# x kept in DRAM between the halves of a feed-forward, its memory used to stage operands; the start of the feed-forward reordered

## The reference

```python
x = x + o @ w_o                                   # end of the cross-attention
h = jnp.square(jax.nn.relu(rms_norm(x, g_f) @ w1))    # w1: 1024 x 4096
return x + h @ w2                                 # w2: 4096 x 1024
```

## Time and profile before

| | |
|---|---|
| median of the runs | 2828.93 us |
| the profiled execution | 2825.01 us |
| its span | 2823.2 us, 51395 instructions |
| TensorE | 2499.7 us busy, 89% |
| VectorE | 1434.8 us busy, 51% |
| ScalarE | 851.6 us, 30% |
| GpSimd | 472.6 us, 17% |
| mean granted clock of TensorE | 0.937 of full |
| feed-forward | from about 2035 to 2806 us of the span |

### The profile page before, as it was taken

The page is one execution under the profiler, slowest core; times in us unless marked ns, Lnnn a source line. Parts: engine busy times, 40 slices in busy tenths (PEclk is TensorE's granted clock), DMA queues, the critical chain, the costliest instruction groups (busy, mean ns, idle before and its releaser), DMA issues. The chain is left out here.

```text
span 2823.2 us, 51395 instructions
## 1 busy us (share of the span) xinstructions
PE 2499.7 (89%) x21934; PEld 2252.0 (80%) x21934; DVE 1434.8 (51%) x2399; ACT 851.6 (30%) x1417; POOL 472.6 (17%) x411
## 2 busy tenths in 40 slices
PE   5998799978996789987999999988879998599888
PEld 5995789837993455556999999976779998599888
DVE  4445566442326677542122324434586765555675
ACT  4324232211124344452121213223332232232332
POOL 1001333203103233210000000000132323122221
PEclk7997899978996999998999999999989999799999
DMA  8320100045112111165111114031024344433432
GB/s 292 104 81 15 18 4 4 4 156 126 41 55 73 45 60 60 60 250 181 46 45 46 45 46 144 8 108 57 23 64 161 127 161 149 165 107 99 153 116 84
DMA packets 181589, 252.81 MB, mean 90 GB/s; under 512 B 19190, under 2 KB 147618, under 8 KB 172681
## 3 DMA queue, kind: packets, MB, share of 16 engines
q1 hardware_dynamic: 170547, 185.53, 21.4%
q0 software_dynamic: 9888, 61.87, 6.2%
q10 hardware_dynamic: 926, 2.12, 0.2%
HBM read 195.56 MB, written 58.28 MB: 90 GB/s over the span
## 5 line engine op out<-in xcount | busy, mean ns | idle before, releaser
L3599 PE MATMUL ps<-ff_operand_high,ff_weight_parts 128*128 128x264 f32 x1024 | 298.6, 292 | 58.7 <-DVE ff_operand_low L3741 19.1
L3601 PE MATMUL ps<-ff_operand_high,ff_weight_parts 128*128 128x264 f32 x1024 | 295.9, 289 | 0.0
L3600 PE MATMUL ps<-ff_operand_low,ff_weight_parts 128*128 128x264 f32 x1024 | 295.8, 289 | 0.0
L3599 PEld LDWEIGHTS ps<-ff_operand_high,ff_weight_parts 128*128 128x128 f32 x1024 | 198.2, 194 | 62.2 <-issue 62.0
L3599 PE MATMUL ps<-ff_sums_high,ff_weight_parts 128*128 128x264 f32 x768 | 221.7, 289 | 27.7 <-DVE ff_hidden L3765 12.5
L3601 PE MATMUL ps<-ff_sums_high,ff_weight_parts 128*128 128x264 f32 x768 | 220.0, 286 | 0.0
L3600 PE MATMUL ps<-ff_sums_low,ff_weight_parts 128*128 128x264 f32 x768 | 219.7, 286 | 0.0
L3600 PEld LDWEIGHTS ps<-ff_operand_low,ff_weight_parts 128*128 128x128 f32 x1024 | 198.4, 194 | 0.0
L3601 PEld LDWEIGHTS ps<-ff_operand_high,ff_weight_parts 128*128 128x128 f32 x1024 | 198.2, 194 | 0.0
L3086 PE MATMUL ps<-xn_h,me_gate_w_high 128*128 128x352 f32 x576 | 186.8, 324 | 6.1 <-DVE me_gate_w_low L3152 6.1
L3087 PE MATMUL ps<-xn_l,me_gate_w_high 128*128 128x352 f32 x576 | 185.5, 322 | 0.0
(11 more groups left out here) (737 smaller groups left out, 6908.0 us busy)
## 6 DMA issues: line engine op xcount, KB each, us to landing
ff_raw<-in_w_ff SPq DMA_DIRECT2D x64, 512.0 KB, 5.1
ff_staged<-hidden_operands SPq DMA_DIRECT2D x28, 1056.0 KB, 5.0
hidden_operands<-ff_hidden SPq DMA_DIRECT2D x16, 1056.0 KB, 4.3
hidden_operands<-ff_hidden_sums SPq DMA_DIRECT2D x16, 792.0 KB, 7.0
me_gate_w_raw<-in_w_in SPq DMA_DIRECT2D x23, 512.0 KB, 3.9
pj_raw<-in_w_in SPq DMA_DIRECT2D x13, 512.0 KB, 4.6
xn_high<-xn_h POOLq DMA_DIRECT2D x1, 4224.0 KB, 14.3
xn_low<-xn_l POOLq DMA_DIRECT2D x1, 4224.0 KB, 25.4
```

The costliest lines, as they stand in the source:

```text
L3599: e.matmul(o[:, cols], wring[:, r, 0, k, :], high(i)[:, k, cols], start=first, stop=False, skip_group_check=True)
L3600: e.matmul(o[:, cols], wring[:, r, 0, k, :], low(i)[:, k, cols], start=False, stop=False, skip_group_check=True)
L3601: mm = e.matmul(o[:, cols], wring[:, r, 1, k, :], high(i)[:, k, cols], start=False, stop=k == 3, skip_group_check=True)
```

## The change

x is stored to DRAM (`x_dram`) in unit 0 of the feed-forward, and its memory becomes four more staging buffers (`x_staged`). Operands 0 to 3 of the down half are loaded into them in unit 8; 4 uses `staged[0]`, 5 and 6 use two of the four again, 7 and later alternate as before. x comes back in four loads (`back`), each when the buffers on it have been converted, and the first group's takes into x wait for them. `hidden_after` gives other places for the conversions. SP issues the staged loads of the group changes before the second weight half of the unit, and the first two of the group after next behind it. Two of the four running tiles of P1's results (`g1`) change place. At the start, the squares of the last 288 columns and their sums are made in `stage_mem` block by block between the output products, as are the rest of the second third's scaling and unit 0's weight sums; VectorE forms all operand sums, and the first half of product 0 no longer waits for the last third.

```diff
-        at = 7 * (NPAIR + 4 * g - 1) + i + 2
-        if n in (1, 2):
-            at += n
-        if n in (3, 4, 5, 6):
-            at = 7 * NPAIR + n - 2
-        if at == q:
+        late = (0, 1, 2, 3, 6, 9, 11) if g == 0 else (0, 1, 3, 5, 7, 8, 10)
+        if 7 * (NPAIR + 4 * g - 1) + late[i] == q:
             out.append(n)
     return out
+
+
+def weight_sums(e, raw, tmp, s_ws, u):
+
+    A = lambda i, j: raw[:, (2 * u + j) % HALVES, :, P * i:P * i + P]
+    e.tensor_tensor(tmp[0][:, :, :], A(1, 0), A(1, 1), ALU.add).then_inc(s_ws, 1)
+    e.wait_ge(s_ws, 4 * u + 1)
+    e.tensor_tensor(tmp[1][:, :, :], tmp[0][:, :, :], A(0, 0), ALU.subtract).then_inc(s_ws, 1)
+    e.tensor_tensor(A(1, 0), A(0, 0), A(1, 0), ALU.subtract).then_inc(s_ws, 1)
+
+
+def weight_last_sum(e, raw, tmp, s_ws, u):
+
+    e.wait_ge(s_ws, 4 * u + 2)
+    e.tensor_tensor(tmp[2][:, :, :], raw[:, (2 * u + 1) % HALVES, :, 0:P], tmp[1][:, :, :], ALU.subtract).then_inc(s_ws, 1)
 
...
-    squares = alloc("end_squares", O, [P, KD, NL])
+    x_staged = [alloc(f"x_staged{b}", at - 4 * KD * T + 16 * NH * b, [P, 4, NH]) for b in range(4)]
...
     t1 = alloc("first_product", K.cst_at + 512, [P, NH])
-    g1 = [outB[:, m, :] for m in range(3)] + [t1[:, :]]
-    tmp = [alloc("weights_s1", K.cst_at + 2656, [P, 4, P]), alloc("weights_s2", K.cst_at + 2656 + 2048, [P, 4, P]),
-           alloc("weights_s4", K.utail_at, [P, 4, P])]
+    g1b = alloc("first_product_sums", slab - 2048 - 4 * NH, [P, NH])
+    g1 = [t1[:, :], g1b[:, :], outB[:, 0, :], outB[:, 1, :]]
...
-    PARTS = (slice(0, 2 * THIRD), slice(2 * THIRD, NH))
-    stage_of = lambda n: 0 if n < 3 else (n - 3) % 2
+    PARTS = (slice(0, 2 * THIRD), slice(2 * THIRD, NH), slice(0, NH))
+    in_x = lambda n: n < 7 and n != 4
+    slot = lambda n: (n if n < 4 else n - 3) if in_x(n) else (0 if n == 4 else n % 2)
+    stage_home = lambda n: x_staged[slot(n)] if in_x(n) else staged[slot(n)]
+    stage_count = lambda n: 16 * (1 + sum(in_x(l) == in_x(n) and slot(l) == slot(n) for l in range(n)))
...
 
             def stage(n):
                 g, i = divmod(n, 7)
-                if n == 0:
+                if n < 4:
+                    e.wait_ge(s_xd, 16)
+                    e.wait_ge(s_n, 1)
+                    e.wait_ge(s_sa[0], 32)
+                    e.wait_ge(s_sa[1], 32)
+                    e.wait_ge(s_sb, 64)
+                elif n == 4:
                     e.wait_ge(s_sa[0], 16 * (NPAIR // 2))
-                elif n == 4:
+                elif n in (5, 6):
+                    e.wait_ge(s_x2, n - 2)
+                elif n == 7:
                     e.wait_ge(s_sa[1], 16 * (NPAIR // 2))
                     e.wait_ge(s_sb, 16 * NPAIR)
-                elif n < 4:
-                    e.wait_ge(s_x2, n)
+                elif n == 8:
+                    e.wait_ge(s_x2, 5)
                 else:
                     e.wait_ge(s_x2, n - 1)
-                e.dma_start(staged[stage_of(n)][:, :, :], kept[:, g, KEPT[i], :, :]).then_inc(s_st[stage_of(n)], 16)
-
+                e.dma_start(stage_home(n)[:, :, :], kept[:, g, KEPT[i], :, :]).then_inc((s_xs if in_x(n) else s_st)[slot(n)], 16)
+
+            def back(m):
+                e.wait_ge(s_x2, (1, 2, 6, 7)[m])
+                e.dma_start(x[:, 2 * m:2 * m + 2, :], xkept[:, 2 * m:2 * m + 2, :]).then_inc(s_xr[m], 16)
+
+            xkept = K.x_dram.rearrange("p (k n) -> p k n", k=KD)
             for u in range(NU):
-                if 1 <= u <= NPAIR:
+                if 1 <= u < NPAIR:
                     store(u - 1)
                 if 2 * u + 3 < 2 * NU:
                     half(2 * u + 3)
+                if u == 0:
+                    e.dma_start(xkept, x[:, :, :]).then_inc(s_xd, 16)
+                if u == 8:
+                    for n in range(4):
+                        stage(n)
+                if u == NPAIR - 1:
+                    stage(4)
+                    back(0)
+                    stage(5)
+                if u == NPAIR:
+                    back(1)
+                    store(NPAIR - 1)
+                if u == NPAIR + 1:
+                    back(2)
+                g, m = divmod(u - NPAIR, 4)
+                if u >= NPAIR and m == 3 and g < 3:
+                    for n in range(7 * (g + 1) + 2, 7 * (g + 2)):
+                        stage(n)
                 if 2 * u + 4 < 2 * NU:
                     half(2 * u + 4)
                 if u == NPAIR - 1:
-                    for n in range(4):
+                    stage(6)
+                if u == NPAIR + 1:
+                    back(3)
+                    stage(7)
+                    stage(8)
+                if u >= NPAIR and m == 3 and g < 2:
+                    for n in range(7 * (g + 2), 7 * (g + 2) + 2):
                         stage(n)
-                if u >= NPAIR:
-                    g, m = divmod(u - NPAIR, 4)
-                    if u == NPAIR:
-                        for n in range(4, 9):
-                            stage(n)
-                    elif m == 3 and g < 3:
-                        for n in range(7 * (g + 1) + 2, min(7 * (g + 2) + 2, 28)):
-                            stage(n)
 
         @block.gpsimd
         def _(e):
...
+                weight_sums(e, raw, tmp, s_ws, u)
                 if u:
...
+                weight_last_sum(e, raw, tmp, s_ws, u)
+
             for u in range(1, NU):
                 sums(u)
 
         @block.tensor
         def _(e):
-            def product(q):
+            def product(q, halves=(0, 1)):
                 u, i = divmod(q, 7)
                 o, r = bank(u, SLOT[i]), q % RINGW
-                for z in range(2):
+                for z in halves:
                     cols = slice(NH // 2 * z, NH // 2 * z + NH // 2)
                     for k in range(4):
                         first = k == 0 and i in (P1, P6, P5)
                         e.matmul(o[:, cols], wring[:, r, 0, k, :], high(i)[:, k, cols], start=first, stop=False, skip_group_check=True)
                         e.matmul(o[:, cols], wring[:, r, 0, k, :], low(i)[:, k, cols], start=False, stop=False, skip_group_check=True)
                         mm = e.matmul(o[:, cols], wring[:, r, 1, k, :], high(i)[:, k, cols], start=False, stop=k == 3, skip_group_check=True)
...
+                    e.wait_ge(s_z, 1)
+                    product(0, (0,))
                 if u == 0:
                     e.wait_ge(s_x1, i + 1)
                 elif u >= NPAIR and (u - NPAIR) % 4 == 0:
                     e.wait_ge(s_x2, 7 * ((u - NPAIR) // 4) + i + 1)
                 room(u, i)
-                product(q)
+                product(q, (1,) if q == 0 else (0, 1))
 
         @block.scalar
         def _(e):
...
                 e.wait_ge(s_mm, 7 * (NPAIR + 4 * g - 1) + i + 1)
-                e.activation(high(i), staged[b][:, :, :], ACT.Copy).then_inc(s_xh2, 1)
-
-            e.activation(squares[:, :, :], x[:, :, end], ACT.Square).then_inc(s_sq, 1)
-            e.wait_ge(s_n, 1)
+                e.activation(high(i), stage_home(n)[:, :, :], ACT.Copy).then_inc(s_xh2, 1)
+
             operand_high(P1, 0)
             weights_high(0)
-            operand_high(P2, 0)
-            weights_high(1)
             e.wait_ge(s_var, 1)
             e.activation(rstd[:, end], rstd[:, end], ACT.Sqrt).then_inc(s_root, 1)
+            operand_high(P2, 0)
             operand_high(P3, 0)
+            weights_high(1)
+            weights_high(2)
+            e.wait_ge(s_n, 1)
+            operand_high(P1, 1)
             e.wait_ge(s_T2, 1)
-            operand_high(P6, 0)
-            operand_high(P5, 0)
+            operand_high(P6, 2)
+            operand_high(P2, 1)
+            e.wait_ge(s_T4, 1)
+            operand_high(P4, 2)
+            operand_high(P5, 2)
             e.wait_ge(s_T3, 1)
-            operand_high(P7, 0)
-            e.wait_ge(s_T4, 1)
-            operand_high(P4, 0)
-            e.wait_ge(s_n, 2)
-            operand_high(P1, 1)
-            weights_high(2)
-            operand_high(P2, 1)
+            operand_high(P7, 2)
             operand_high(P3, 1)
-            e.wait_ge(s_TB, 1)
-            for i in (P6, P7, P5, P4):
-                operand_high(i, 1)
 
             for q in range(NQ):
                 u, i = divmod(q, 7)
...
@@ -3809,6 +3831,8 @@
                         e.drain()
                     return
                 v = u - NPAIR
+                if g == 0 and i == P6:
+                    e.wait_ge(s_xr[m], 16)
                 if i == P5:
                     e.wait_ge(s_td, 7 * v + P7 + 1)
                 elif i == P3:
...
 
-            for k in range(4, KD):
-                mm = normed_third(e, K, xn, x, rstd, 1, k)
-            e.drain().then_inc(s_n, 1)
+            def first_sum(to, a, b, z):
+                c = PARTS[z]
+                return e.tensor_tensor(whole(to)[:, :, c], whole(a)[:, :, c], whole(b)[:, :, c], ALU.subtract)
+
+            first_sum(P5, P7, P1, 0)
```

(60 more changed lines are left out.)

44 lines of the change are left out of this document (13 added, 31 removed).

## The result

The changed kernel took 2781.06 us (median of 4 runs, 2777.24 to 2785.46) and the kernel before 2827.44 (4 runs, 2824.36 to 2832.48). The ratio is 0.9835, 95% interval 0.981 to 0.9859. It is faster by 46; 2770 was forecast. The profiled execution took 2777.24 against 2825.01.

A forecast was written before the change was run, and what follows sets the result against it. TensorE was taken to be 89% busy, leaving only idle and half-clock time. Head 3, unit 8 -1, seam 36 and group changes 19 sum to 57 off 2825, 2768 profiled, given as 2770; range 2756 to 2792 for 8 in 10.

The forecast's parts named there:

- What bounds the kernel: TensorE 89% busy, only idle and half-clock time winnable; at three seam and group-change waits VectorE stood at conversions lacking staged operands.
- Seam: Between up and down halves, units 15 to 17: staging in x's memory cuts the excess from 50.2 to 14, gain 36 us.
- rival 2: Seam and head: GpSimd's weight sums block VectorE's conversions for whole sets; seam gain 27, head's gone, 2780; chance 0.14.
- Head: Feed-forward's start: sums moved ahead and a shorter VectorE chain up to the first unit's P4 product; gain 3 us.
- Unit 8: Middle of the up half: four loads of 1056 KB fill the queue, so GpSimd's weights come late; loss 1 us.
- Group changes: Three later changes in the down half: earlier, spread conversions remove the gap, a late weight half remains at two; gain 19 us.
- Rival 1: Group changes: late loads make conversions slip in the two buffers' cycle, so no gain there; 2787 to 2789; chance 0.13.
- Rival 3: Down units: weight halves stand behind staged loads and x's blocks in the queue, starving weights; slower, 2840; chance 0.03.
- Rival 4: Unit 8: late stores of the group or x hold up its loads in SP; time as Rival 3, no chance of its own.

The follow-up runs named there:

- e1_no_x: Changed kernel without x's way to DRAM and back; all operands staged in the two buffers at the earlier places: 2808.52 us, ratio 0.994.
- e4_filled: Changed kernel with matmuls nobody reads put into five of TensorE's waits, before products 2, 5, 108, 114 and 118: 2772.13 us, ratio 0.9803.
- e6_spread: Changed kernel with the four loads into x's memory issued one each in units 5 to 8, not all in unit 8: 2784.53 us.
- e11_guarded: Changed kernel with the loads into x's memory two each in units 7 and 8, issued once GpSimd has begun the next unit's weight sums: 2781.25 us.
- e8_tuned: Changed kernel with e2_order's queue order, e6_spread's loads, and one conversion later at the seam and in later groups: 2769.37 us, ratio 0.9797.
- e2_order: Changed kernel with the first two staged loads of the group after next issued one unit later, behind that unit's weight halves: 2773.86 us, ratio 0.9808.
- e7_old_places: Changed kernel with e2_order's queue order, but the later groups' conversions at the places of the kernel before: 2797.38 us.
- e9_all: Changed kernel with e2_order's order, e8_tuned's later conversions, e11_guarded's loads and unread matmuls in five TensorE waits: 2753.56 us, ratio 0.9757.

## Why the prediction was right, point by point

The forecast time of 2770 is 11 under the measured one, within the range, and the sign and, in the main, the mechanism were right. By its own steps:

**What bounds the kernel.** Right for the most part. The idle time at the seam was mainly VectorE at conversions whose operand had not landed; e1_no_x, which keeps all but that staging, is back at 83.0 of 91.05. One of the three readings was wrong. Behind the 15.86 VectorE did not stand at a conversion but, for 11.36 us, at the take of P1, whose tile was still being stored (the row of 2432.64). The change frees that tile, and this is worth the other 8.0; the prediction has no term for it and put the whole gain down to the staging.

**Seam, 36, measured 34.7.** The written order followed gave releases at 2387.3, 2397.7, 2409.6 and 2423.4; measured 2387.39, 2399.15, 2412.05 and 2427.66, waits of 9.85 us in all against 9.4. The excess over 40.8 is 15.5: the 9.85, three falls of the clock at 1.5 where one at 1.6 and 3 us of GpSimd were charged, and 1.1 that shows as neither. That the sum came out is in part luck: GpSimd's part was smaller than its term (its 1.1 is within the 9.85) and the clock's larger. GpSimd did stretch VectorE. These rows are VectorE's, kernel after, a conversion alone and one beside GpSimd, then the two GpSimd sums that met it:

```profile
2384.28 2.35 DVE L3770 TENSOR_TENSOR ff_operand_low<-ff_x_staged,ff_operand_high 128x2112 fp32r<-128x2112 f32 x1
...
2394.95 3.44 DVE L3770 TENSOR_TENSOR ff_operand_low<-ff_x_staged,ff_operand_high 128x2112 fp32r<-128x2112 f32 x1
```

```profile
2394.55 1.62 POOL L3452 TENSOR_TENSOR ff_weights_s<-ff_weights_s,ff_raw 128x512 f32<-128x512 f32 x1
2396.14 3.39 POOL L3453 TENSOR_TENSOR ff_raw<-ff_raw 128x512 f32<-128x512 f32 x1
```

The conversion took 1.1 more, less than one GpSimd sum, and the second GpSimd sum took 3.39 for 1.3: each waited for the other once. The Trainium skill (SBUF — State Buffer, "Who interferes with whom") says that the two exclude each other; these rows agree, 3.44 us for 2.35 and 3.39 for 1.3. What didn't come is a whole set of 6 us ahead of one conversion. So rival 2's place was right and its price was not.

**Head, 3, measured 0.8.** By its share the step that failed most; in microseconds the largest miss is at the group changes, below. Its chain was sized well: from the block's start at 2038.04 (forecast 2038.5) to the release at 2079.72 it took 41.7 us against 40.5, with the stretched sums gone (1.6 for 1408 elements, first rows below) and a last one still stretched beside GpSimd (3.44 for 2.35; the weight part ahead of it took 1.77 for 0.7):

```profile
2038.04 1.63 DVE L3847 TENSOR_TENSOR ff_sums<-xf_scaled 128x1408 f32<-128x1408 f32 x1 [1.58 <-PEq L3907]
2039.95 1.62 DVE L3764 TENSOR_TENSOR ff_operand_low<-xf_scaled,ff_operand_high 128x1408 fp32r<-128x1408 f32 x1
...
2075.51 3.44 DVE L3764 TENSOR_TENSOR ff_operand_low<-xf_scaled,ff_operand_high 128x2112 fp32r<-128x2112 f32 x1
```

That is 1.2 of the 2.2 missing. The rest is mostly the clock. Behind the wait of 2.48 comes a product at half clock, and from the release to P1's take in unit 1 it is 10.55 us, where the kernel before, at full clock behind its 2.69, took 9.03: 1.5 for which 0.6 was charged. e4_filled took 1.5 back.

**Unit 8, -1, measured -1.3 over the stretch (-1.8 in the two units; -2.8 over the stretch in the second trace).** The size was about right, the reason not quite. The loads took a median of 13.7 us to land against the 5.0 of the earlier trace rows, but GpSimd's weights came late because the half ahead of them was slowed in flight, as e6_spread and e11_guarded show.

**Group changes, 19, measured 12.7.** The mechanism was right, but a wait was missing. As forecast, two changes keep a wait before the second product of the unit after, released by a weight part (4.32 and 4.29 against 5.0), and the third has none. What the prediction overlooked is that a product also needs its output bank. Product 139, a P3, goes to the bank of product 137, the P5 of the same unit; it can't start until VectorE has taken that one, and the take stands behind the third conversion. VectorE's rows, kernel after:

```profile
2488.21 3.08 DVE L3770 TENSOR_TENSOR ff_operand_low<-ff_staged,ff_operand_high 128x2112 fp32r<-128x2112 f32 x1 [0.29 <-ACT ff_operand_high L3712]
2491.21 0.69 DVE L3843 TENSOR_TENSOR x<-x,ps 128x528 f32<-128x528 f32 x1
```

The take ends at 2491.9 and the matmul of 2492.05 follows. With this wait the unit takes 22.07 instead of 20.40, at each of three changes: 3 x 1.67 = 5.0 of the 6.3 us missing. The prediction compared only the conversions with the products. It also overlooked GpSimd here: its weight sums fall on this third conversion at all three changes, which took 3.08, 3.32 and 3.39 us for 2.35. That would make 0.7 to 1.0 of the 1.27 rival 2's mechanism in another place; no run tests it. And e8_tuned, which has the conversion one product later, got only 0.5 to 0.8 of the 1.67 back. The clock behind the 4.3 cost 1.5 for 1.0, which those waits, 0.7 shorter than forecast, make good. The other 1.3 are short waits: 0.3 us at each of the first two changes, 0.75 and 0.34 at the third, whose second unit took 21.98, with what the profile doesn't show as idle. Rival 1, the buffers' cycle, was at most a small part: ScalarE waited 0.52, 0.27 and 0.20 us for the load of that third operand, and e2_order reaches 63.6 with that cycle, where 61.2 is the floor.

**Rival 3** (starved weights) didn't come: away from the changes the down units run at 20.4, as before. **Rival 4** neither: unit 8's loads are issued at 2239.71, 1.2 us behind the weight half.

## What to carry to other kernels

When engines run written orders, follow each order by hand with durations of the trace, and check every thing that a product waits for: operands, weights and also the bank that an earlier take must free. A transfer that is off the path can still slow one in flight, here by 2 us, so try issuing it after the urgent ones have landed, not after they were issued. Where a buffer's cycle and a queue's order both stand in the way, a fix of one alone can measure as nothing, as e7_old_places did; test them together before you drop either.

## What the runs showed of the hardware

**A short wait can cost more than itself.** Waits of TensorE of 2.06, 2.48 and 2.64 us were followed by a product at 1.2 GHz for the most part, which cost about 1.5 us each. This is no fixed rule by length. In the kernel before the product behind 2.69 us, and in e4_filled the one behind 2.26, ran at 1.00, while in e9_all the one behind 2.46 began at 0.55, though TensorE had been busy for all of the 52.1 us ahead. It isn't even fixed for one kernel: where the kernel after waited 2.64 at 2387.39, its second trace has a wait of 2.49 at 2402.77, and the product behind it ran at 1.00. Windows of before, of the kernel after's second trace, then of e9_all:

```profile
2076.10:2079.10 3.00, 2.99 (x24) 3.00 (x25) 3.00 (x4) 0.00 (x0) 1.90 (x1) 1.00 0.05 18
```

```profile
2402.80:2405.70 2.90, 2.90 (x24) 2.90 (x25) 2.90 (x3) 1.24 (x1) 0.00 (x0) 1.00 1.00 284
```

```profile
2393.50:2396.40 2.90, 2.90 (x14) 2.90 (x15) 2.90 (x3) 0.00 (x0) 2.07 (x2) 0.55 1.05 398
2338.90:2391.00 52.10, 52.10 (x430) 51.89 (x429) 40.98 (x46) 22.63 (x29) 15.82 (x11) 1.00 0.57 190
```

Why the one falls and the other doesn't stays open. Matmuls nobody reads, put into the waits, kept the clock at 1.00 over e4_filled's seam.

**Loads slow one another in flight:** 9.3 us from issue to use of a weight half became 11.6 and 11.3 with one and with four loads of 1056 KB issued behind it.

**The start varies more than the change of a part:** nearly the same work ahead of the feed-forward ended within a span of 24.5 us over thirteen executions, and 14 us apart in two of the same kernel.

**Two engines stretch each other's instructions:** a VectorE conversion of 2.35 us took 3.08 to 3.44 beside GpSimd's sums, and a GpSimd sum of 1.3 took 3.39.
